# Second gate of the hybrid mixing block: eight projection chunks as two groups of seven half-size products

## The reference

```
h = rms_norm(x, norm_mix)
z = h @ w_in                                  # 512 x 4352; q, k, v of both attentions, g_a, g_b
...
gates = sigmoid(concat([g_a, g_b]) + b_gate)  # g_a, g_b: 1024 features each
merged = gates[..., :1024] * (y_a @ w_proj_a) + gates[..., 1024:] * (y_b @ w_proj_b)
x = x + merged @ w_out
h2 = rms_norm(x, norm_mlp)
x = x + square(relu(h2 @ w_up)) @ w_down
```

## Time and profile before

| what | value |
|---|---|
| median of 3 runs | 1081.48 us |
| span of the profiled execution (first to last instruction) | 1079.8 us |
| PE busy | 1071.6 us, 99% |
| DVE busy | 764.1 us, 71% |
| ACT busy | 547.1 us, 51% |
| mean granted TensorE clock | 0.999 |

### The profile page before, as it was taken

The page is one execution under the profiler, slowest core; times in us unless marked ns, Lnnn a source line. Parts: engine busy times, 40 slices in busy tenths (PEclk is TensorE's granted clock), DMA queues, the critical chain, the costliest instruction groups (busy, mean ns, idle before and its releaser), DMA issues.

```text
span 1079.8 us, 14177 instructions
## 1 busy us (share of the span) xinstructions
PE 1071.6 (99%) x5092; PEld 858.6 (80%) x5092; DVE 764.1 (71%) x1296; ACT 547.1 (51%) x930; POOL 158.6 (15%) x257
## 2 busy tenths in 40 slices
...
GB/s 234 142 68 101 79 98 88 118 117 89 44 95 23 76 108 106 98 59 59 107 88 99 78 79 98 86 90 140 192 1 116 215 1 113 200 1 107 146 1 79
DMA packets 30486, 103.65 MB, mean 96 GB/s; under 512 B 3408, under 2 KB 4304, under 8 KB 30416
## 3 DMA queue, kind: packets, MB, share of 16 engines
...
...
## 4 chain that ended last, share of the span: by engine, by line
PE 97%; DVE 1%; ACT 1%; DMA 0%; issue 0%; DVEq 0%; ACTq 0%
PE ps L951 25%; PE ps L953 24%; PE ps L952 24%; PE ps L914 5%; PE ps L913 5%; PE ps L912 5%; PE ps L1062 3%; PE ps L1090 2%; PE ps L1123 2%; PE ps L1117 1%; PE ps L862 1%; DMA raw<-wst 0%; PE ps L989 0%; PE ps L1023 0%; DVE xtok L2001 0%
## 5 line engine op out<-in xcount | busy, mean ns | idle before, releaser
L951 PE MATMUL ps<-xgh,wh 128*128 128x512 f32 x847 | 335.4, 396 | 0.5 <-DVE wl L1494 0.3
L953 PE MATMUL ps<-xgh,wl 128*128 128x512 f32 x847 | 330.2, 390 | 0.0
L952 PE MATMUL ps<-xgl,wh 128*128 128x512 f32 x847 | 329.9, 389 | 0.0
L1494 DVE TENSOR_TENSOR wl<-raw,wh 128x1024 fp32r<-128x1024 f32 x146 | 183.8, 1259 | 50.4 <-ACT wh L1162 49.3
L1162 ACT ACTIVATE wh<-raw 128x1024 fp32r<-128x1024 f32 x146 | 153.0, 1050 | 84.6 <-PE ps L953 64.6
L951 PEld LDWEIGHTS ps<-xgh,wh 128*128 128x128 f32 x847 | 159.0, 188 | 38.7 <-issue 7.0
L953 PEld LDWEIGHTS ps<-xgh,wl 128*128 128x128 f32 x847 | 159.0, 188 | 33.7
L952 PEld LDWEIGHTS ps<-xgl,wh 128*128 128x128 f32 x847 | 159.2, 188 | 32.0 <-issue 0.2
L1373 ACT ACTIVATE Pt<-Pt,stat 128x256 f32<-128x256 f32 (+2 forms) x128 | 64.3, 503 | 99.3 <-DVE stat L1770 40.2
L912 PE MATMUL ps<-wh,fh 128*128 128x512 f32 x224 | 87.1, 389 | 0.0
L913 PE MATMUL ps<-wl,fh 128*128 128x512 f32 x224 | 87.1, 389 | 0.0
...
## 6 DMA issues: line engine op xcount, KB each, us to landing
raw<-wst SPq DMA_DIRECT2D x146, 512.0 KB, 3.4
b<-wdn SPq DMA_DIRECT2D x32, 512.0 KB, 6.9
...
gx<-xT SPq DMA_DIRECT2D x3, 512.0 KB, 6.6
outT<-xtok SPq DMA_DIRECT2D x3, 512.0 KB, 2.6
...
```

Source lines behind the costliest of these rows:

```text
L951: e.matmul(o, high, a, start=(k == 0), stop=False)
L952: e.matmul(o, high, b, start=False, stop=False)
L953: done = e.matmul(o, low, a, start=False, stop=stop)
L1494: e.tensor_tensor(wl_t[:, v % NHL, :], src, f32(wh_t[:, v % NHL, :]), ALU.subtract).then_inc(lo_done, 1)
```

## The change

The eight chunks of the second gate no longer stand between the `pb` chunks. All eight `pb` chunks come first (32 tiles), ACT copies them out of PSUM into a buffer `pbr`, and then come two groups ("octets") of four gate chunks each. A group is a block product: weights in 2x2 blocks (two of four chunks by 512 of 1024 input features), activations in 2x2 blocks (512 input features by 256 tokens), with seven products P1, P5, P6, P2, P7, P3, P4. Each product is 24 matmuls of 128x128 weights by 256 tokens. P1, P6, P7 and P4 go one after the other into one bank, adding to what stands there; between them ACT copies the bank out (P1, P6) and DVE adds (P7). P5 and P3 share a second bank, P2 has a third.

The sums of activations (M1, T3, M2, T4) and their high and low parts are new work for DVE and ACT (`normal_x`, `form_sums`, `forms_low`, `forms_high`). Of the weight sums, DVE makes those for P6 and P3 in `ww`; those for P5 and P7 come from memory: SP loads one block (`wt`, `wu`), and a POOL DMA adds another block to it on landing (`accum_op`). The outputs go through tanh in two halves of 256 per block, since two chunks with different biases share a block. The order of `wc` changes from a group of four split at step 7 to a group of four split at step 4.

```
+OCT = ("P1", "P5", "P6", "P2", "P7", "P3", "P4")
+OCT_BANK = {"P1": "X", "P6": "X", "P7": "X", "P4": "X", "P5": "Y", "P3": "Y", "P2": "Z"}
+OCT_FORM = {"P1": "B11", "P5": "M1", "P6": "M2", "P2": "B21", "P7": "T3", "P3": "B22", "P4": "T4"}
+OCT_ADD = {"P2": 0, "P7": 1, "P3": 2}
+OCT_COPY = {"P1": (0, 0), "P5": (2, 1), "P6": (1, 2)}
+OCT_OUT = (("P2", 0, 0, 0), ("P7", 2, 1, 2), ("P3", 0, 1, 1), ("P4", 2, 0, 2))
+FORMS_HIGH = ("B11", "M1", "B22", "B21", "T3", "M2", "T4")
+LOW_DVE, LOW_LATE = ("B11", "M1", "B22", "B21", "M2"), ("T3", "T4")
...
+    def octet(self, o, x, y, z):
+
+
+        for part, b in (("X", x), ("Y", y), ("Z", z)):
+            self.take_in(("oc", o, part), b)
+        for p in OCT:
+            name = ("oc", o, p)
+            self.bank[name] = self.bank["oc", o, OCT_BANK[p]]
+            for i in range(4):
+                self.tiles.append((name, i, i == 3))
+            self.end[name] = len(self.tiles) - 1
+            self.unit(("ring" if p in ("P1", "P2", "P4") else "sum", o, p), 4)
...
-    ch.one(("z", 26), KD)
-    ch.one(("z", 27), KD)
-    ch.ring = 7
-    for j in range(KD):
-        ch.one(("pb", j), 4)
-        if j < 6:
-            ch.one(("z", 28 + j), KD)
-    ch.seq([("wc", j) for j in range(KD)], KD, 4, 7)
+    for j, b in enumerate((2, 3, 4, 0, 1, 5, 6, 2)):
+        ch.take_in(("pb", j), b)
+    for j in range(5):
+        ch.run(("pb", j), 0, 3, 4)
+    for j in range(5):
+        ch.run(("pb", j), 3, 4, 4)
+    for j in range(5, KD):
+        ch.run(("pb", j), 0, 4, 4)
+    ch.unit(("ring",), UT)
+    ch.octet(0, 3, 4, 0)
+    ch.octet(1, 1, 5, 6)
+    for j, b in enumerate((2, 3, 4, 0, 5, 6, 1, 2)):
+        ch.take_in(("wc", j), b)
+    for j in range(4):
+        ch.run(("wc", j), 0, 4, KD)
+    for j in range(4):
+        ch.run(("wc", j), 4, KD, KD)
+    for j in range(4, KD):
+        ch.run(("wc", j), 0, KD, KD)
...
+            elif p[0] == "pb":
+                q.wait_ge(pbc_done, p[1] + 1)
+            elif p[0] == "oc" and p[2] == "X":
+                q.wait_ge(og_done, 8 * p[1] + 8)
+            elif p[0] == "oc":
+                q.wait_ge(oa_done, 3 * p[1] + {"Y": 3, "Z": 1}[p[2]])
...
+        def sum_there(q, o, p):
+
+            if p == "P5":
+                q.wait_ge(wt_sum, 16 * (o + 1))
+                return wt
+            if p == "P7":
+                q.wait_ge(wu_sum, 16 * (o + 1))
+                return wu
+            q.wait_ge(ww_done, 2 * o + (1 if p == "P6" else 2))
+            return ww
...
+            if oct_no[0, "P1"] <= u < oct_no[1, "P4"] + 1 + NHL:
+                UNIT_AT[u] = max(ch.units[u - NHL][2] + 2.0, UNIT_AT[u - 1] + 3.6)
...
+        FORM_AT = step_at["prod", 31, 1] + 2.2
+        SUM_AT = {"m1": 5.6, "t3": 9.4, "n2": 14.0, "s2": 21.0, "T3": 16.2, "t4": 18.4, "s4": 32.5, "T4": 23.0}
+        HIGH_AT = {"B11": 5.2, "M1": 7.6, "B22": 10.2, "B21": 12.0, "T3": 13.7, "M2": 16.0, "T4": 20.4}
+        SUM_B = {"s2": UNIT_AT[oct_no[0, "P3"]] + 3.5, "s4": UNIT_AT[oct_no[1, "P6"]] + 3.5}
...
+                        old = ch.units[ring[w - NRAW]][0]
+                        if len(old) == 3 and old[2] != "P4":
+                            q.wait_ge(ww_done, 2 * old[1] + (1 if old[2] == "P1" else 2))
...
+            def gate_sums():
+
+                for o in range(2):
+                    yield FORM_AT if o == 0 else FORM_AT + SUM_AT["s2"] + 3.0
+                    q.wait_ge(ol_done, 8)
+                    if o:
+                        unit_split(q, oct_no[0, "P5"])
+                        q.wait_ge(ww_done, 1)
+                    e.dma_start(wt, woc[o, 1]).then_inc(wt_in, 16)
+                    yield FORM_AT + 0.5 if o == 0 else UNIT_AT[oct_no[0, "P7"]] + 4.0
+                    if o:
+                        unit_split(q, oct_no[0, "P7"])
+                    e.dma_start(wu, woc[o, 0]).then_inc(wu_in, 16)
...
+                if i == 0 and p in ("P6", "P7", "P3"):
+                    q.wait_ge(vc_done, 3 * o + {"P6": 1, "P7": 3, "P3": 2}[p])
+                if i == 0 and p == "P4":
+                    q.wait_ge(oa_done, 3 * o + 2)
+                opens = p in ("P1", "P5", "P2")
+                half = i // 2
+                out_ = bank[ch.bank[name]][:, 256 * half:256 * half + 256]
+                for k in (2 * (i % 2), 2 * (i % 2) + 1):
+                    w = slice(512 * half + 128 * k, 512 * half + 128 * k + 128)
+                    x = slice(256 * k, 256 * k + 256)
+                    e.matmul(out_, wh_t[:, v % NHL, w], high[:, x], start=(i == 0 and k == 0 and opens), stop=False, skip_group_check=True)
+                    e.matmul(out_, wh_t[:, v % NHL, w], low[:, x], start=False, stop=False, skip_group_check=True)
+                    done = e.matmul(out_, wl_t[:, v % NHL, w], high[:, x], start=False, stop=(i == 3 and k == 3), skip_group_check=True)
+                done.then_inc(tile_done, 1)
...
+            def octet_copies(o):
+                for p in ("P1", "P5", "P6"):
+                    v, n = OCT_COPY[p]
+                    name = ("oc", o, p)
+                    yield ev_at[name]
+                    q.wait_ge(tile_done, end[name] + 1)
+                    q.wait_ge(ol_done, 8)
+                    if o:
+                        q.wait_ge(mb_done, {"P1": 1, "P5": 4, "P6": 3}[p])
+                    e.activation(vb[v], bank[ch.bank[name]], ACT.Copy).then_inc(vc_done, 1)
+
+            def octet_gates(o):
+                for n in range(4):
+                    p = OCT_OUT[n][0]
+                    cs, _, v = out_block(o, n)
+                    yield ev_at["oc", o, p] + (1.2 if n < 3 else 0.1)
+                    if n < 3:
+                        q.wait_ge(oa_done, 3 * o + n + 1)
+                        src = v
+                    else:
+                        q.wait_ge(tile_done, end["oc", o, p] + 1)
+                        q.wait_ge(mb_done, 4 * o + 2)
+                        src = bank[ch.bank["oc", o, p]]
+                    for i in range(2):
+                        c = HBG + 8 + cs.start + i
+                        e.activation(v[:, 256 * i:256 * i + 256], src[:, 256 * i:256 * i + 256], ACT.Tanh,
+                                     scale=-0.5 if n % 2 else 0.5, bias=drvc(c, c + 1)).then_inc(og_done, 1)
...
+            def normal_x():
+                for k in range(KD):
+                    yield FORM_AT + 1.1 * k
+                    q.wait_ge(ol_done, 8)
+                    q.wait_ge(rstd_done, 3)
+                    e.scalar_tensor_tensor(hz[:, k, :], xt[:, k, :], P_("mix_g", k), rstd, ALU.mult, ALU.mult).then_inc(hz_done, 1)
...
+            def gate_adds(o):
+                yield FORM_AT + SUM_AT["s2"] if o == 0 else SUM_B["s2"]
+                q.wait_ge(wt_sum, 16 * (o + 1))
+                w = ring_no[oct_no[o, "P1"]]
+                raw_there(q, w)
+                if o:
+                    unit_split(q, oct_no[0, "P3"])
+                e.tensor_tensor(ww, wt, raw_t[:, w % NRAW, :], ALU.add).then_inc(ww_done, 1)
+                yield FORM_AT + SUM_AT["s4"] if o == 0 else SUM_B["s4"]
+                w = ring_no[oct_no[o, "P2"]]
+                raw_there(q, w)
+                unit_split(q, oct_no[o, "P6"])
+                q.wait_ge(ww_done, 2 * o + 1)
+                e.tensor_tensor(ww, ww, raw_t[:, w % NRAW, :], ALU.add).then_inc(ww_done, 1)
...
+            def octet_adds(o):
+                for n in range(3):
+                    p = OCT_OUT[n][0]
+                    _, _, v = out_block(o, n)
+                    yield ev_at["oc", o, p]
+                    q.wait_ge(tile_done, end["oc", o, p] + 1)
+                    q.wait_ge(vc_done, 3 * o + (1, 2, 3)[n])
+                    e.tensor_tensor(v, bank[ch.bank["oc", o, p]], v, ALU.add).then_inc(oa_done, 1)
...
+            def merge_b(o):
+                for n in range(4):
+                    cs, half, v = out_block(o, n)
+                    yield ev_at["oc", o, OCT_OUT[n][0]] + 2.4
+                    q.wait_ge(og_done, 8 * o + 2 * n + 2)
+                    q.wait_ge(pbc_done, cs.stop)
+                    e.scalar_tensor_tensor(two(v), two(v), 1.0, pbr[:, cs, half], ALU.add, ALU.mult).then_inc(om_done, 1)
+                    yield ev_at["oc", o, OCT_OUT[n][0]] + 2.7
+                    q.wait_ge(om_done, 4 * o + n + 1)
+                    q.wait_ge(ev_done, ev_no(("pa", 7)))
+                    e.tensor_tensor(mg[:, cs, half], mg[:, cs, half], two(v), ALU.add).then_inc(mb_done, 1)
...
+            def gate_sums(o):
+                yield FORM_AT + 5.0 if o == 0 else FORM_AT + SUM_AT["s2"] + 10.0
+                q.wait_ge(wt_in, 16 * (o + 1))
+                e.dma_start(wt, woc[o, 2], accum_op=ALU.add).then_inc(wt_sum, 16)
+                yield FORM_AT + 5.1 if o == 0 else UNIT_AT[oct_no[0, "P7"]] + 9.0
+                q.wait_ge(wu_in, 16 * (o + 1))
+                e.dma_start(wu, woc[o, 1], accum_op=ALU.add).then_inc(wu_sum, 16)
```

(33 more changed lines are left out.)

185 lines of the change are left out of this document (144 added, 41 removed).

## The result

| | time, median | runs |
|---|---|---|
| kernel before | 1081.47 us | 4 (1081.34 to 1081.59) |
| changed kernel | 1087.31 us | 4 (1086.82 to 1087.48) |

The ratio is 1.0053, 95% interval 1.0039 to 1.0067: the change makes the kernel 5.8 us slower. The forecast was 1086.2. The profiled execution has a span of 1085.7 us.

A forecast was written before the change was run, and what follows sets the result against it. PE, busy 99% of the span, was taken as the bound. A gain of 3.2 us against waits of 1.5, 2.6, 2.4, 1.0 and four restarts of 0.1 gave +4.7: 1081.5 becomes 1086.2 us, range 1080.2 to 1094.

The forecast's parts named there:

- The product's pitch: Matmuls of 256 columns in a product start 0.12 us apart on PE; 336 take 40.3 us, a gain of 3.2.
- First wait: PE waits 1.5 us before the first group's P6 for ACT's copy of P1's bank.
- Second wait: PE waits 2.6 us before the first group's P4; DVE's output sum stands behind a weight sum awaiting the accumulating DMA.
- X: Time of POOL's accumulating DMA, taken as 6 us between bounds of 3.4 and 10.3.
- Third wait: PE loses 2.4 us before the second group's P6, waiting for ACT's copy of P1's bank.
- a sign of mine that failed: A PE gap was to show before P6 of both groups, put down to ACT's copy of the bank.
- Fourth wait: PE loses 1.0 us before the second group's P4, since three weight splits keep DVE from P2's output.
- Nothing behind the stage: From `wc`'s start to the end the length stays as before; only the `raw` buffer a unit uses changes.
- it takes long: Rival: accumulating DMA takes 10.3 us, DVE is held until 674.9, 4.3 us more, 1090.5 us; chance 0.14.
- DVE becomes nearly full, and its order decides: DVE's queue between last attention output and last `ml` holds 64.4 us of work in about 68.
- the 4.8 us of an output block: Each output block costs the loop of ACT and DVE steps 4.8 us, against products of 2.88.
- The waits as a sum: The four PE waits of 1.5, 2.6, 2.4 and 1.0 us were added, with 0.1 for each restart.

The follow-up runs named there:

- e_loads_later: Changed kernel with SP's `raw` and `wu` loads held until the second group's accumulating DMA has landed; 1085.9 us.
- e_fill: Changed kernel plus 17 matmuls of 512 columns, into a bank nobody reads, in PE's gap before the first group's P4; 1087.7 us.
- e_orders: Changed kernel with the second group's weight sum later, first group's P1 bank copy early, weight splits 0.5 tick earlier, `mh` and `ml` later; 1079.0 us.
- e_splits: Changed kernel with the stage's weight splits on ACT and DVE 0.5 tick earlier; 1081.9 us.
- e_sum_copy: Changed kernel with the second group's weight sum behind two output sums on DVE and ACT's first-group copy of P1's bank early; 1083.1 us.
- e_sum_splits: Changed kernel with the second group's weight sum behind the output sums on DVE and the weight splits earlier; 1080.2 us.

## Why the prediction was right, and where it was off

- **The product's pitch**, 0.12: right to the digit; gain 3.3, forecast 3.2.
- **First wait**, 1.5 and 0.1 for the restart: 1.6 measured. ACT's copy ended at 663.28 (forecast 663.4).
- **Second wait**, 2.6 and 0.1: 4.1. T4 was there at 658.35 (forecast 658.3), POOL could issue at 664.7 (664.6), but the DMA took X = 7.2, not 6: 1.2 of the 1.4 missing. I had counted reading and writing the target, not the `raw` and `wu` loads that SP sends 0.6 and 1.7 us behind it (e_loads_later: 5.6 without them).
- **Third wait**, 2.4 and 0.1: no gap in the changed kernel, a sign of mine that failed, and still no error of the sum: e_fill shows the wait at 2.6. What the prediction lacked is that the granted clock fell to 1.2 GHz behind PE's gap of 4.2 us. That used up the same time, because ACT's copy ends at 690.1 to 690.2 either way.
- **Fourth wait**, 1.0 and 0.1: 0.7.
- **Nothing behind the stage**: right, 380.1 us in both.
- **The step that was mis-sized** is X in the second wait, put at 6 us from bounds of 3.4 and 10.3: -3.3 + 1.6 + 4.1 + 2.6 + 0.7 = +5.7 against my +4.7. The rival "it takes long" had the right sign of it, at 10.3 too large.
- **"DVE becomes nearly full, and its order decides"**: the second half was the true one. DVE was busy 54 of the 67 us from 637 to 704 in the changed kernel, 64 in e_orders, which is faster. I took the 4.8 us of an output block as its cost; it held 1 us of waiting that another order fills (3.85 in e_splits).
- **The waits as a sum**: they gave the total because each is measured from where the last one left PE. As prices of repairs they are wrong. Repairing the first one is worth 0.35 us while the output blocks set the pace (e_sum_copy) and 1.2 when they no longer do (e_orders against e_sum_splits). Repairing the order of the splits gave 5.4, part of it by the DMA's side effect.
